# The recurrent gates of a two-block network on one core: border products on stacked activations, groups spread between chunks

## The reference

```python
h = rmsnorm(x, norm_g)
u = h @ w_in                                  # 1024 x 3072
xb, gate = u[..., :1536], u[..., 1536:]
xb = causal_depthwise_conv(xb, conv_w, conv_b)            # 4 taps
xs = xb.reshape(bsz, seq, 16, 96)
r = sigmoid(einsum('bshi,hij->bshj', xs, wr) + br)        # 16 blocks of 96 x 96
i = sigmoid(einsum('bshi,hij->bshj', xs, wi) + bi)
log_a = -8 * r * softplus(-lam)
a = exp(log_a)
b = sqrt(-expm1(2 * log_a)) * (i * xb)
hs = associative_scan(a, b)                               # along the tokens
y = hs * silu(gate)
return x + y @ w_out
```

## Time and profile before

| | |
|---|---|
| Median of 3 runs | 792.99 us (792.81 to 792.99) |
| The profiled execution | 792.79 us |
| Its span, first to last instruction | 791.0 us |
| PE / PEld busy | 782.8 us (99%) / 717.9 us (91%) |
| DVE / ACT / POOL busy | 581.2 us (73%) / 489.5 us (62%) / 83.5 us (11%) |
| Chain that ended last | PE 95%, DVE 2%, ACT 2%, DMA 1% |
| Granted PE clock | 0.999 |

### The profile page before, as it was taken

One profiled execution on the slowest core, in us unless ns is written; L12 is line 12 of the kernel. 1 busy time (PEld: TensorE's weight loads), 2 busy tenths in 40 slices (PEclk: granted clock), 3 DMA queues, 4 the chain that ended last, 5 costly groups with the idle time before them and its releaser, 6 DMA issues.

```text
span 791.0 us, 14668 instructions
## 1 busy us (share of the span) xinstructions
PE 782.8 (99%) x5381; PEld 717.9 (91%) x5381; DVE 581.2 (73%) x884; ACT 489.5 (62%) x763; POOL 83.5 (11%) x150
## 2 busy tenths in 40 slices
PE   8999999999999999999999999999999999999997
PEld 7999999998998888888888899999999888888885
DVE  5986897978967877786449665696578787787443
ACT  7779956878765655554346475764756655555434
POOL 9405100058100000000000021000000000000000
PEclk9999999999999999999999999999999999999999
DMA  8724566533546666665665554346555666665651
GB/s 271 224 80 125 170 194 207 177 119 109 175 143 186 199 193 193 190 185 202 191 187 165 181 161 152 116 140 181 164 167 171 182 206 203 187 186 184 189 184 53
DMA packets 101045, 136.30 MB, mean 172 GB/s; under 512 B 5065, under 2 KB 86401, under 8 KB 100993
## 3 DMA queue, kind: packets, MB, share of 16 engines
q1 hardware_dynamic: 99232, 133.23, 55.8%
q0 software_dynamic: 1600, 2.28, 1.1%
q10 hardware_dynamic: 160, 0.07, 0.0%
HBM read 134.51 MB, written 1.05 MB: 171 GB/s over the span
## 4 chain that ended last, share of the span: by engine, by line
PE 95%; DVE 2%; ACT 2%; DMA 1%; issue 0%; SPq 0%; ACTq 0%
PE bank L557 35%; PE bank L620 20%; PE bank L622 11%; PE bank L565 8%; PE bank L666 8%; PE bank L713 5%; PE bank L714 3%; PE bank L884 1%; PE bank L866 1%; PE bank L891 1%; DVE w_lo L1665 1%; ACT acts L1157 1%; DMA arena<-x 1%; PE bank L894 0%; ACT w_hi L1157 0%; DVE acts L1703 0%
## 5 line engine op out<-in xcount | busy, mean ns | idle before, releaser
L1665 DVE TENSOR_TENSOR w_lo<-stage,w_hi 128x1024 fp32r<-128x1024 f32 x249 | 304.0, 1225 | 133.9 <-ACT w_hi L1157 133.2
L1157 ACT ACTIVATE w_hi<-stage 128x1024 fp32r<-128x1024 f32 (+1 forms) x251 | 262.5, 1050 | 118.3 <-PE bank L557 41.1
L557 PE MATMUL bank<-acts,w_hi 128*128 128x256 f32 x1584 | 288.7, 284 | 0.4 <-DVE acts L1766 0.2
L557 PEld LDWEIGHTS bank<-acts,w_hi 128*128 128x128 f32 x1584 | 246.5, 192 | 2.6 <-issue 1.7
L620 PE MATMUL bank<-acts,w_hi 128*128 128x512 f32 x704 | 245.2, 392 | 0.0
L557 PE MATMUL bank<-acts,w_lo 128*128 128x256 f32 x792 | 224.0, 283 | 0.0
L622 PE MATMUL bank<-acts,w_lo 128*128 128x256 f32 x704 | 197.2, 280 | 0.0
L620 PEld LDWEIGHTS bank<-acts,w_hi 128*128 128x128 f32 x704 | 131.7, 187 | 29.1
L557 PEld LDWEIGHTS bank<-acts,w_lo 128*128 128x128 f32 x792 | 151.8, 192 | 0.0
L622 PEld LDWEIGHTS bank<-acts,w_lo 128*128 128x128 f32 x704 | 133.1, 189 | 0.0
L1157 ACT ACTIVATE arena<-bank 128x512 f32<-128x512 f32 (+1 forms) x79 | 43.6, 561 | 64.6 <-PE bank L622 47.7
(11 more groups left out here) (201 smaller groups left out, 764.5 us busy)
## 6 DMA issues: line engine op xcount, KB each, us to landing
stage<-ffn_w_gate SPq DMA_DIRECT2D x44, 512.0 KB, 4.5
stage<-ffn_w_up SPq DMA_DIRECT2D x44, 512.0 KB, 4.6
stage<-ffn_w_down SPq DMA_DIRECT2D x44, 512.0 KB, 3.8
stage<-w_in SPq DMA_DIRECT2D x40, 512.0 KB, 3.7
stage<-a_w_in SPq DMA_DIRECT2D x24, 512.0 KB, 4.7
stage<-b_w_in SPq DMA_DIRECT2D x16, 512.0 KB, 3.8
stage<-a_w_out SPq DMA_DIRECT2D x12, 512.0 KB, 3.6
stage<-b_w_out SPq DMA_DIRECT2D x8, 512.0 KB, 3.6
```

The source lines that it names most:

```text
L557: mm = pe.matmul(dst, w[:, slot, c:c + P], a[:, k, :] if isinstance(k, int) else a[:, bass.ds(k, 1), :], start=start and n == 0, stop=stop ...
L1157: return nc.scalar.activation(out_, in_, func, **kw)
L1665: dve.tensor_tensor(w_lo[:, n % RING, 0:w], src, w_hi[:, n % RING, 0:w].bitcast(F32), ALU.subtract)\
```

## The change

- **Border products.** Of a group's seven tile products per half, the three with output tile = input tile stay and take three passes (`GATE_MAIN`). The four that cross a border touch only 32 or 64 input rows each. Their input rows are stacked with high parts beside low parts in one tile per output tile (`stacked`, twelve tiles), and the weights of those rows are laid twice under one another (`GATE_AGAIN`, 16 more POOL transfers). One product with `w_hi` then gives w_hi on a_hi and w_hi on a_lo, and one with `w_lo` the third pass: two products per output tile (`GATE_REST`).
- **Stacking.** Eight transfers per group from SBUF to SBUF on SP's queue, placed between the weight loads; SP waits for `xbl`, PE for `stack_in`.
- **Gate halves** have 768 columns instead of 896.
- **Order.** Group 1 stands after x chunk 4, group 2 after gate chunk 0, group 3 after gate chunk 1. Gate chunk 2 goes to bank 0.
- **Tangents.** sigmoid(v) is taken as (1 + tanh(v / 2)) / 2; the factors go into the biases, into lambda and the square root's scale.
- **ACT's order.** Decays 0 to 2 stand inside the loop over halves, at 14, 16 and 20; lambda's exponential moves from 7 to 2.
- **DVE's order.** It takes the product of i and x from POOL; lambda's steps start six halves earlier; two gate chunk copies, products and squares stand inside the loop.
- **Places.** `x_tok` and `gate_hi` swap their arena regions.

```diff
-GATE_TILES = [(0, 0, 0), (1, 0, 256), (0, 1, 128), (1, 1, 384), (2, 1, 640), (1, 2, 512), (2, 2, 768)]
+GATE_MAIN, GATE_REST = [0, 512, 256], [384, 128, 640]
+GATE_AGAIN = [(1, 32, 64, 64, 384 + 96, 0, 32), (1, 0, 32, 64, 128, 32, 64),
+              (2, 64, 32, 32, 128 + 64, 0, 64), (2, 0, 64, 0, 640, 64, 32)]
+STACK = [(1, 0, 32, 0, 2, 0), (1, 96, 32, 0, 0, 96), (1, 32, 32, 1, 2, 0), (1, 64, 32, 1, 0, 96),
+         (0, 0, 64, 0, 1, 0), (0, 64, 64, 1, 1, 0), (2, 64, 64, 0, 1, 64), (2, 0, 64, 1, 1, 64)]
-H_RI = [8, 14, 16, 18]
+H_RI = [8, 12, 18, 22]
...
+            def stack(g):
+
+                sp.wait_ge(xbl, (3 * g + 2) // 2 + 1)
+                for m, p, n, part, k, at in STACK:
+                    sp.dma_start(stacked(g, m)[p:p + n, :].bitcast(F32), acts[at:at + n, 8 + 3 * g + k, part, :].bitcast(F32)).then_inc(stack_in[g], 16)
...
-            stream(C_G, 6, lambda j: col(w_in, j + 6))
+            stack(0)
+            load(C_G, col(w_in, 6), split(C_G - 2))
+            stack(1)
+            load(C_G + 1, col(w_in, 7), split(C_G - 1))
+            load(C_G + 2, col(w_in, 8), split(C_G))
+            stack(2)
+            load(C_G + 3, col(w_in, 9), split(C_G + 1))
+            stack(3)
+            stream(C_G + 4, 2, lambda j: col(w_in, j + 10))
...
                 for w in range(2):
                     half = H_RI[g] + w
                     pe.wait_ge(w_done, half + 1)
...
+                    for m, c in enumerate(GATE_MAIN):
+                        dst, first = place(w, m)
+                        passes(dst, half % RING, c, 8 + 3 * g + m, first, False)
+                pe.wait_ge(stack_in[g], 16 * len(STACK))
+                for w in range(2):
+                    half = H_RI[g] + w
+                    for m, c in enumerate(GATE_REST):
+                        dst, _ = place(w, m)
+                        pe.matmul(dst, w_hi[:, half % RING, c:c + P], stacked(g, m), start=False, stop=False,
+                                  skip_group_check=True)
+                        mm = pe.matmul(dst, w_lo[:, half % RING, c:c + P], stacked(g, m), start=False, stop=True,
+                                       skip_group_check=True)
                     mm.then_inc(ring_free, 1)
...
-                    gates(0)
-            for g in range(1, LG):
-                gates(g)
+                if c in (3, 4):
+                    gates(c - 3)
...
                 col_chunk(C_G + c, gate_bank(c))
+                if c < 2:
+                    gates(2 + c)
...
-            for n in range(half_of(C_G)):
+            for n in range(half_of(C_G + 2)):
                 if n - 1 in x_end:
                     xb_hi(x_end[n - 1])
-                if n == 7:
+                if n == 14:
+                    act.wait_ge(lam_ready, 1)
+                if n in (14, 16, 20):
+                    decay((14, 16, 20).index(n))
+                if n == 2:
                     f(lam[:, 0, :], par_a[:, LAM:LAM + LT], ACT.Abs).then_inc(lam_e, 1)
...
-                        y = f(tiles((RR, II)[w] + t), b[:, (q % 2) * T:(q % 2 + 1) * T], ACT.Sigmoid,
+                        y = f(tiles((RR, II)[w] + t), b[:, (q % 2) * T:(q % 2 + 1) * T], ACT.Tanh, scale=0.5,
...
-            for g in range(LG):
-                decay(g)
-                hi(24 + g)
+            decay(3)
+            hi(28)
...
+                if n in (half_of(C_G) + 2, half_of(C_G + 1) + 2):
+                    gate_out((n - half_of(C_G)) // 4)
...
+                if n == 19:
+                    lru_gated(0)
+                if n == 20:
+                    lru_gated(1)
+                if n == 21:
+                    lru_square(0)
+                if n == 22:
+                    lru_square(1)
+                if n == 23:
+                    lru_gated(2)
...
-            lo(24)
-            gate_out(0)
-            lru_square(0)
-            lo(25)
-            lru_square(1)
-            lo(26)
-            gate_out(1)
+            lru_gated(3)
             lru_square(2)
-            lo(27)
             gate_out(2)
+            lo(28)
             lru_square(3)
-            lo(28)
```

More of the change, by code:

```diff
@@ L145, in gate_bank @@
 def gate_bank(c):
[L147 removed]
+    return (4, 5, 0, 4, 5, 7)[c]
 def mix_bank(c):
@@ L244, in build @@
         stage_in = [sem(f"stage_in{q}") for q in range(4)]
-        gate_in = [sem("gate_in0"), sem("gate_in1")]
+        gate_in, stack_in = [sem("gate_in0"), sem("gate_in1")], [sem(f"stack_in{g}") for g in range(LG)]
         set_done = sem("set_done")
@@ L394, in stream @@
                 j = 0
-                while j < n and chunk + j < C_G + 2:
-                    load(chunk + j, view(j), split(chunk + j - 2) if chunk + j >= 2 else None)
-                    j += 1
                 turns = (n - j) // 2
@@ L472, in _ @@
                             .then_inc(gate_in[pair], 16)
+                for w, name in enumerate(("a_gate_r_w", "a_gate_i_w")):
+                    blocks = I[name][0].rearrange("(g b) i j -> b i g j", b=4)
+                    for b, r, n, p, c, j0, jn in GATE_AGAIN:
+                        pool.dma_start(place[p:p + n, :, w, c:c + jn],
+                                       blocks[b, r:r + n, 2 * pair:2 * pair + 2, j0:j0 + jn]).then_inc(gate_in[pair], 16)
             for first, name, n in ((F1_G, "ffn1_norm_2", KD), (MIX_G, "mix_norm_2", KD), (F2_G, "ffn2_norm_2", KD),
@@ L756, in gates, with place @@
                 banks = ((0, 1, 2), (3, 6, 7))[g % 2]
+                pe.wait_ge(xbl, (3 * g + 2) // 2 + 1)
+                if g == 1:
+                    pe.wait_ge(par_ready, 2)
+                if g >= 2:
+                    pe.wait_ge(ri_sig, 2 * (g - 1))
+                def place(w, m):
+                    q = 3 * w + m
+                    return bank[banks[q // 2]][:, (q % 2) * T:(q % 2 + 1) * T], q % 2 == 0
                 for w in range(2):
@@ L1265, in _, with decay @@
             gate_end = {H_RI[g] + 1: g for g in range(LG)}
-            for n in range(half_of(C_G)):
+            def decay(g):
+                act.wait_ge(ri_sig, 2 * g + 1)
+                for m in range(3):
+                    t = 3 * g + m
+                    s = f(tiles(AA + t), tiles(RR + t), ACT.Exp, scale=lam[:, 7, t:t + 1],
+                          bias=lam[:, 7, t:t + 1])
+                s.then_inc(lru_a, 1)
+                for m in range(3):
+                    t = 3 * g + m
+                    s = f(tiles(RR + t), tiles(RR + t), ACT.Tanh, scale=lam[:, 7, t:t + 1],
+                          bias=lam[:, 7, t:t + 1])
+                s.then_inc(lru_t, 1)
+            for n in range(half_of(C_G + 2)):
                 if n - 1 in x_end:
                     xb_hi(x_end[n - 1])
-                if n == 7:
+                if n == 14:
[3 more added lines that the diff above has]
+                if n == 2:
                     f(lam[:, 0, :], par_a[:, LAM:LAM + LT], ACT.Abs).then_inc(lam_e, 1)
```

93 lines of the change are left out of this document (38 added, 55 removed).

## The result

| | before | after |
|---|---|---|
| Median of the runs | 792.99 us | 797.87 us (796.72 to 799.11) |
| Ratio after / before | | 1.0063, 95% interval 1.0052 to 1.0073 |
| Profiled execution / its span | 792.79 / 791.0 us | 797.76 / 795.9 us |
| Granted PE clock | 0.999 | 0.995 |

The profiled spans differ by 4.9 us, like the medians. One execution of the kernel before took 2621.01 us and is left out of the ratio. The page of the changed kernel first (the last line is a group: PE's passes with a high part, with the idle time ahead of them and what ended it); it answers to the earlier trace rows.

A forecast was written before the change was run, and what follows sets the result against it. PE was taken as the bound, one unbroken chain at 0.1204 us per product. 48 fewer save 5.78 us, less 2.1 us of waits for stack 0 and half 20: -3.7, median 789.3 us, own range 788.3 to 790.6.

The forecast's parts named there:

- The term for stack 0: Group 0's stacked transfers: eight issues of 0.37 us on SP, landing in 4.7 us, costing PE a 0.7 us wait.
- rival (d): Slower: stacks land in 7.2 us; group 0 waits 3.2, group 1 1.0, group 3 3.4; 795.2 us, chance 0.08.
- the sentence apart: Stack landings by the Trainium skill's DMA rule: 2.2 us for 64 KB, every stack in time, loss 1.65 us.
- The decays: ACT's decays inside the loop over halves: each group's six instructions priced at 2.4 us.
- The wait for half 20: PE behind group 2 waits for DVE's low half of gate chunk 1: 1.65 us, 1.4 once stack 0 is late.
- rival (c): PE's clock drops to 1.2 GHz after the half 20 wait, losing half of 3.8 us: 791.2 us, chance 0.04.
- the rule that I set beside it: Trainium skill's rule on PE's clock: pauses between bursts throttle PE again, making the clock the case to fear.
- Half 29 closest, 0.7 us before its need: After half 20, the closest low part is half 29's, 0.7 us before PE needs it; before the change 0.9.
- the sum: Saving of 5.78 us less 2.1 us of waits for stack 0 and half 20: net -3.7 us.
- nothing on the path: POOL's 16 more issues at 0.63 us, 10 us in all, land before they are wanted and cost PE nothing.
- Every product removed is worth its pace, as long as the weights still arrive in time: PE's stretch from 17.81 us: 48 products fewer at 0.1204 us each save 5.78 us.
- my walk: ACT, DVE and PE stepped through the new order with trace durations; the old order came within 0.3 us up to 60 us.

The follow-up runs named there:

- split_queue: Changed kernel with four of the eight transfers of group 0's stack issued by POOL instead of SP; 794.44 us.
- decay_later: Changed kernel with decay 1 moved on ACT from half 16 to half 18; 797.14 us.
- padded: early_all with 12 dummy passes at the head of each gate group, giving PE its 48 products back; 794.71 us.
- early_all: split_queue with stack 1 before gate chunk 0's loads, decay 1 at half 18, halves 28 and 29 and group 2's product drawn forward; 793.39 us.
- lo28_first: Changed kernel with half 28's low part ahead of group 2's square in DVE's order; 796.59 us.
- late_all: all_three with halves 28 and 29 and group 2's product drawn forward, and stack 2 issued one load earlier; 794.65 us.
- square_on_dve: early_all with POOL's four squares of a done by DVE; 794.65 us.
- late_first_group: Changed kernel with gate groups 0 and 1 each one x chunk later; 794.65 us.
- all_three: late_first_group with decay 1 moved to half 18 and half 28's low part ahead of group 2's square; 795.55 us.
- fill_right: Changed kernel with 13 dummy PE products in the wait for stack 0 and 10 behind group 2; 795.92 us.
- tangent_no_bias: Changed kernel without the bias of the decays' tangents, square root replaced by a copy, results not the kernel's; run once, 797.18 us.
- fill_both: Changed kernel with 25 dummy PE products in the wait for stack 0 and 20 behind group 2; 798.65 us.

## Why the prediction was wrong

**Right.** 48 products fewer, and a stacked product at full clock has the pace of the others, 0.120 us. The chain breaks at half 20, PE waiting for DVE's low part directly after group 2, two decays ahead of it. The first wait is for stack 0. The products of y come in time: PE waits for none. The transfers that POOL issues are on no path.

**The term for stack 0** was mis-sized. "Each stack is 8 issues of 0.37, 3 us" took a load from memory for a transfer from SBUF to SBUF: 5.2 us passed from the first start to the last, not 2.6. The landing, on which I spent the bounds, was 4.4 against my 4.7. The wait of 3.1 is close to the 3.2 that rival (d), at 0.08, gave group 0, but by luck: (d) had the sign and this place, through a landing of 7.2 us that never came, and its waits of 1.0 for stack 1 and 3.4 for group 3 did not come either. split_queue shows the issues: four less on SP, 2.5 us less wait. The 2.2 us of the sentence apart on the stacks is close to the least of the 32 landings, 2.0; the median was 3.1, and stack 0's last took 4.37.

**The decays** were priced 2.4, start to start, from a row without the bias operand; they take 2.95 (3.07 less overlap). The wait for half 20 came out at 2.43, not 1.4, and at 68.2 us instead of 63.3; decay_later, with one decay moved, has none there.

**The clock.** I gave rival (c) one fall, at half 20, and 0.04. There were two, each 1.5 us, about 2 us net. The waits behind which they came, 3.1 and 2.4, were mis-sized as 0.7 and 1.4: the first two errors brought this one. The trace agrees with the rule that I set beside it, from the Trainium skill, TensorE: Matmul & The Clock Gate, section "HAM oscillation", in that the clock fell behind pauses; but behind pauses of 2.49 and 3.27 us in other runs it did not.

**"Half 29 closest, 0.7 us before its need"** failed. Half 28 was 0.84 late and half 29 0.54, and neither is in the sum. I had POOL "nothing on the path" by looking at its issues, while its squares of a held DVE for 1.43 us and stretched two of its steps by 1.2 each. Moreover the margin was that of a walk in which nothing upstream was late.

Together, in the terms of the sum: stack 0 +2.4 us, half 20 +1.0, halves 19, 28 and 29 +1.6, two falls +3.0, short gaps +0.5, which is 8.5 of the 8.6 between -3.7 and +4.9.

**The deepest step**, behind all these, was the first: "Every product removed is worth its pace, as long as the weights still arrive in time." I wrote the condition, and tested it at four places against my walk. The profile of before had a warning in one view that I did not read for it: ACT at 19.94 of 20 us from 80 to 100. PE never waited there, but its feeders were nearly as slow. Removing or moving any one of the waits found above only moved it to the next half (half 20 to 24 and 28, 28 to 29, 29 to 30 and 32), and padded shows that in early_all's order 1.3 of the 5.78 us reach the end. For the old order this is argued and not shown: no run takes the 48 products away and leaves the order of ACT and DVE as it was. The best of the versions, early_all, is level with the kernel before; none beats it.

**Open.** How ACT and DVE could be made shorter here was not tried beyond moving the squares. Nor was the copy of half 30 moved. decay_later is 1.3 us longer than its ledger: 0.5 of it passed ahead of the stretch, whose first product starts at 18.28 us instead of 17.81, and 0.7 in gaps too short to be counted, as in the other runs. And what besides its length decides whether a wait brings the clock down is not known.

## What to carry to other kernels

Where one engine is at 99% and the engines that feed it are at 90% or more over the same 20 us, a cut on the first may be worth no more than the slack of the others: read the busy time by stretch, feeders included, before multiplying instructions saved by their pace. Test it with the reverse: give the engine dummy work and see whether the time follows. And price a new kind of transfer or operand by its own form, since small pieces in a row on one queue cost by the issue (here 0.6 us each), and put them on two queues or well before their want.

## What the runs showed of the hardware

- A transfer from SBUF to SBUF of 32 or 64 rows costs SP 0.59 us to issue (0.55 to 1.30), a weight load of 512 KB 0.37. It lands in 2.0 to 4.4 us in the changed kernel.
- Falls of the clock to 1.2 GHz come in or shortly behind waits of PE (from 0.9 us ahead of the wait's end in lo28_first to 1.4 behind it in decay_later), but the wait's length alone does not tell: a fall of 3.41 us came behind waits of 1.92 (late_all), 2.15 (split_queue), 2.43 and 3.11 us (after), 3.10 (decay_later) and in one of 3.55 (square_on_dve), one of 6.83 in 3.12 (lo28_first), and none behind 2.39 (decay_later, at 37.7 us), 2.49 (late_first_group), 2.47 (lo28_first, at 96 us) or 3.27 (all_three). What else decides, these runs leave open. A fall of 3.41 us takes 1.5 us of PE's time, and cost between nothing (late_all) and about 1 us each (fill_right) at the end.
- An operand that holds a bias per partition adds 0.093 us to an ACT instruction of 256 columns (tangent_no_bias).
- VectorE's two low parts of 128 x 1024 took 3.62 us beside GpSimd's squares (early_all) and 2.35 with GpSimd silent (square_on_dve).
- A `matmul` of 128 fp32 columns on ones took 0.223 us, nearly twice a pass of 256 columns of the kernel's own; the trace has two products for each (fill_both).
